# Attention's running sums over seven block pairs, with suffix sums on GpSimd, and late modulation sums on column quarters

## The reference

```python
z = einsum('bhqd,bhkd->bhqk', qb, kb) * scale
strict = s_idx < t_idx
log_keep = where(strict, log_sigmoid(-z), 0.0)
later = cumsum(log_keep, axis=3, reverse=True) - log_keep
att = where(strict, exp(log_sigmoid(z) + later), 0.0)
```

## Time and profile before

| what | value |
|---|---|
| median of 3 runs | 1100.38 us |
| lowest and highest run | 1097.2 and 1100.89 us |
| span of the profiled execution | 1095.7 us, 4.7 us below the median |
| TensorE, VectorE, ScalarE, GpSimd busy | 94, 61, 30 and 15% of the span |
| mean granted clock of TensorE | 0.994 of full speed |
| traffic with HBM | 254 GB/s over the span |

### The profile page before, as it was taken

The page is one execution under the profiler, slowest core; times in us unless marked ns, Lnnn a source line. Parts: engine busy times, 40 slices in busy tenths (PEclk is TensorE's granted clock), DMA queues, the critical chain, the costliest instruction groups (busy, mean ns, idle before and its releaser), DMA issues.

```text
span 1095.7 us, 18202 instructions
## 1 busy us (share of the span) xinstructions
PE 1028.6 (94%) x7403; PEld 591.1 (54%) x7403; DVE 665.0 (61%) x1131; ACT 326.2 (30%) x500; POOL 167.4 (15%) x220
## 2 busy tenths in 40 slices
PE   3999999999999999999998999999999999889895
PEld 1588588755557677768884444444334333333332
DVE  2478768444457443238347777777776665666666
ACT  4342462366652223365351111111111101110114
POOL 0100000322220011264500200000000000001003
PEclk9999999999999999999999999999999999999998
DMA  9676303205320004243439999999999999999994
GB/s 342 245 242 217 136 28 127 77 13 180 115 77 2 3 4 157 72 155 123 172 122 407 376 396 401 400 402 399 407 404 408 404 404 395 405 396 402 411 423 196
DMA packets 67732, 275.22 MB, mean 251 GB/s; under 512 B 7742, under 2 KB 17256, under 8 KB 43098
## 3 DMA queue, kind: packets, MB, share of 16 engines
q1 hardware_dynamic: 62976, 263.84, 62.4%
q10 hardware_dynamic: 2218, 6.52, 1.6%
q0 software_dynamic: 2480, 4.01, 1.3%
HBM read 274.26 MB, written 4.21 MB: 254 GB/s over the span
## 4 chain that ended last, share of the span: by engine, by line
PE 45%; SPq 25%; DVE 13%; DMA 7%; ACT 5%; issue 3%; POOL 1%; DVEq 0%; ACTq 0%
SPq L476 17%; PE ps L2211 8%; SPq L480 5%; PE ps L2230 4%; PE ps L1878 3%; DMA ring<-in_w_in 3%; DMA arena<-in_w_up 2%; SPq L484 2%; PE ps L2195 2%; PE ps L1859 2%; DMA arena<-in_w_mod 2%; PE ps L1867 2%; PE ps L1979 2%; PE ps L1860 1%; PE ps L1861 1%
## 5 line engine op out<-in xcount | busy, mean ns | idle before, releaser
L1544 DVE TENSOR_TENSOR arena<-arena,ps 128x1024 f32<-128x1024 f32 x124 | 145.5, 1215 | 52.9 <-PE ps L2195 52.9
L2211 PE MATMUL ps<-arena 128*64 128x512 f32 x672 | 152.9, 596 | 12.0 <-DMA arena<-in_w_up 11.2
L2211 PEld LDWEIGHTS ps<-arena 128*64 128x64 f32 x672 | 47.5, 137 | 105.5 <-issue 99.8
L1054 ACT ACTIVATE results<-ps,ST 64x512 fp32r<-64x512 f32 x64 | 43.8, 685 | 182.8 <-PE ps L2230 182.4
L2211 PE MATMUL ps<-ring,arena 128*64 128x512 f32 x352 | 79.9, 597 | 6.9 <-DMA ring<-in_w_up 5.5
L1047 ACT ACTIVATE arena<-ps 128x256 f32<-128x256 f32 x32 | 12.3, 385 | 234.7 <-PE ps L2211 234.7
L1720 PE MATMUL ps<-h_upper,w_upper 128*128 128x512 f32 (+1 forms) x184 | 73.7, 401 | 4.8 <-POOL h_lower_first L604 4.6
L2230 PE MATMUL ps<-arena 128*64 128x512 f32 x336 | 76.7, 598 | 1.3 <-DMA arena<-in_w_down 1.3
L1554 DVE SCALAR_TENSOR_TENSOR results<-ps,ST,results 64x512 fp32r<-64x512 f32 x64 | 48.0, 749 | 47.4 <-ACT results L1054 46.9
L2195 PE MATMUL ps<-results,back 128*128 128x512 f32 x248 | 73.7, 419 | 0.0
L1722 PE MATMUL ps<-h_upper,w_lower 128*128 128x512 f32 (+1 forms) x184 | 72.1, 392 | 0.0
(11 more groups left out here) (424 smaller groups left out, 1866.7 us busy)
## 6 DMA issues: line engine op xcount, KB each, us to landing
arena<-in_w_up SPq DMA_DIRECT2D x84, 1024.0 KB, 28.1
ring<-in_w_up SPq DMA_DIRECT2D x44, 1024.0 KB, 27.7
ring<-in_w_down SPq DMA_DIRECT2D x11, 2048.0 KB, 32.4
arena<-in_w_down SPq DMA_DIRECT2D x11, 2048.0 KB, 31.4
arena<-in_w_down SPq DMA_DIRECT2D x20, 1024.0 KB, 27.2
ring<-in_w_mod SPq DMA_DIRECT2D x6, 2048.0 KB, 9.1
arena<-in_w_mod SPq DMA_DIRECT2D x6, 2048.0 KB, 9.5
ring<-in_w_in SPq DMA_DIRECT2D x6, 2048.0 KB, 8.4
```

Source lines behind the costliest of these rows:

```text
L1544: TT(two_banks(acc[:, t, :]), two_banks(acc[:, t, :]), ps[:, BACK_BANK[t]:BACK_BANK[t] + 2, :], ALU.add).then_inc(back_added, 1)
L2211: last = mm(ps[64 * hf:64 * hf + 64, UP_BANK, :].rearrange("p (m n) -> p m n", m=2), hgT[:, k, :], up_pair(u, k)[:, :, 256 * hf:256 * hf + ...
```

## The change

Running sums. After the masks, GpSimd adds to the off-diagonal part of key block 2 the block 3, and to that of block 1 the new block 2 (`suffix_sums`), each after a wait for its own instruction before. Then block 1 holds, for the queries behind it, the sum of blocks 1 to 3. `sums` needs only the pair (`j`, `j`) and the next one: for `j` = 0 with `nones` on block 1, for `j` = 1 and 2 with a third matrix `-before` (-1 where the row lies strictly ahead of the column), which takes off what the triangular product of the enlarged block counted too much. Seven pairs, 14 products per head. ScalarE makes the third matrix from the constants.

Late modulation. Each accumulator is multiplied with 32 columns of ones only, into a quarter of 32 partitions of one of two banks; VectorE copies both banks to `late_rows`; TensorE, between the first two parts of Gram group 0, turns them by eight transposes of 128x128; VectorE picks every 32nd column and adds the bias in two small additions, after the first three steps of group 0. The separate addition of the bias goes away.

```diff
-        tri_r = sb("tri_r", [P, 2, P], F32R)
+        tri_r = sb("tri_r", [P, 3, P], F32R)
...
+        late_rows = acc_l[0:2]
...
-        LATE_BANK = (2, 3, 4, 5, 2, 3, 2, 3)
+        LATE_BANK = (2, 3)
...
+            def suffix_sums(buf, h):
+
+                for j, step in ((2, 1), (1, 2)):
+                    pool.wait_ge(sp_added, 2 * h + step)
+                    v, n = buf[:, OFF[j] + P:OFF[j] + WID[j]], WID[j + 1]
+                    nc.gpsimd.tensor_tensor(v, v, buf[:, OFF[j + 1]:OFF[j + 1] + n], ALU.add).then_inc(
+                        sp_added if step == 1 else sp_masked, 1)
...
-                    diag(e_buf[i], sp_masked)
+                    diag(e_buf[i], sp_added)
+                    suffix_sums(e_buf[i], 2 * p + i)
...
-            A(tri_r[:, 1, :], K("nones"), ACT.Copy).then_inc(lora_tri, 1)
+            A(tri_r[:, 1, :], K("nones"), ACT.Copy)
+            A(tri_r[:, 2, :], K("before"), ACT.Copy, scale=-1.0).then_inc(lora_tri, 1)
...
-            own = eb[:, 0:2048].rearrange("p (j q n) -> p j q n", j=4, q=4)
-            dve.wait_ge(av_all, NH)
-            for j in range(NH):
-                dve.wait_ge(lcol_done, j + 1)
-                TT(own[:, j % 4], ps[:, LATE_BANK[j], :].rearrange("p (q n) -> p q n", q=4),
-                   K("ident").rearrange("p (o n) -> p o n", o=1).broadcast_to((P, 4, P)), ALU.mult).then_inc(lcol_evac, 1)
-                dve.wait_ge(lcol_evac, j + 1)
-                ins = nc.vector.tensor_reduce(modc[:, 4 * j:4 * j + 4].rearrange("p (q o) -> p q o", o=1), own[:, j % 4], AX, ALU.add)
+            dve.wait_ge(lcol_done, 2)
+            for b in range(2):
+                CP(late_rows[b], ps[:, LATE_BANK[b], :]).then_inc(lcol_evac, 1)
+
+            def late_sums_in():
+
+                dve.wait_ge(lcol_done, 3)
+                turned = psf[:, 512 * LATE_BANK[0]:512 * LATE_BANK[0] + 1024].rearrange("p (b q c x) -> p b q c x", b=2, q=4, x=32)
+                of = lambda a: a.rearrange("p (b c q) -> p b q c", b=2, c=4)
+                for b in range(2):
+                    ins = TT(of(modc)[:, b], turned[:, b, :, :, 0], of(V("bl", 0, 32))[:, b], ALU.add)
+                ins.then_inc(lcol_evac, 1)
...
-                link(TT(modc, modc, V("bl", 0, 32), ALU.add))
+                dve.wait_ge(lcol_evac, 3)
...
+                if f == 0:
+                    late_sums_in()
...
-                    for jj in range(j, NT):
+                    for jj in range(j, min(j + 2, NT)):
                         o = 1536 * (h % 2) + OFF[j] + P * (jj - j)
+                        left = 0 if jj == j else (1 if j == 0 else 2)
                         for sp in (sp_hi[h % 2], sp_lo[h % 2]):
-                            last = mm(psf[:, o:o + WID[jj]], tri_r[:, 0 if jj == j else 1, :],
+                            last = mm(psf[:, o:o + WID[jj]], tri_r[:, left, :],
...
-            def late_sum(j):
-                if j >= 4:
-                    earlier = max(i for i in range(j) if LATE_BANK[i] == LATE_BANK[j])
-                    pe.wait_ge(lcol_evac, earlier + 1)
-                mm(ps[:, LATE_BANK[j], :], K("ones"), acc_l[j], start=True, stop=True).then_inc(lcol_done, 1)
-
-            for j in range(6):
-                late_sum(j)
+            for b in range(2):
+                for q in range(4):
+                    last = mm(ps[32 * q:32 * q + 32, LATE_BANK[b], :], K("ones")[:, 0:32], acc_l[4 * b + q], start=True, stop=True)
+                last.then_inc(lcol_done, 1)
...
-                        pe.wait_ge(lcol_evac, NH)
+                        pe.wait_ge(lcol_evac, 3)
...
-                    late_sum(6)
-                    late_sum(7)
+                    for b in range(2):
+                        pe.wait_ge(lcol_evac, b + 1)
+                        for q in range(4):
+                            last = tr(ps[:, LATE_BANK[b], P * q:P * q + P], late_rows[b][:, P * q:P * q + P], ident)
+                    last.then_inc(lcol_done, 1)
```

More of the change, by code:

```diff
@@ L321, in build @@
         tok_src, tr_done, tr_act, tr_dve = sem("tok_src"), sem("tr_done"), sem("tr_act"), sem("tr_dve")
-        sp_rounded, sp_split = sem("sp_rounded"), sem("sp_split")
+        sp_rounded, sp_split, sp_added = sem("sp_rounded"), sem("sp_split"), sem("sp_added")
         z_done, log_ready, sp_ready, sp_masked, cum_done, att_ready, att_masked, av_all, ysb_ready = (
```

## The result

The changed kernel takes 1104.63 us (median), the kernel before 1099.6 us beside it: a ratio of 1.0048, with a 95% interval of 1.0034 to 1.0062. It is slower by 5 us, where 1.6 us less was forecast, and outside the range. The profiled execution has a span of 1099.8 us.

A forecast was written before the change was run, and what follows sets the result against it. Bound: chains of waits in attention and behind it, carried one to one through the expert stage. Attention +2.6 and late modulation -4.2 give -1.6 us, a span of about 1094.1; applied to the median, 1098.8 us, range 1095.6 to 1102.8.

The forecast's parts named there:

- TensorE's clock falls: Rival, attention: 2.1 us idle before the second head's sums halves the clock, 10.4 us more in four pairs, 1109; chance 0.07.
- The adds: Attention, GpSimd: two adds per head put 1.16 us (0.98 to 1.35) on the second head's chain, nothing on the first's.
- the upper row: Attention, GpSimd: 2.1 ns per column plus 0.19 us per start gave 1.19 us for both adds; 1.0 was taken.
- the proportion to one larger instruction: Attention, GpSimd: scaling the 128x512 in-place product (1.09 us) to 384 columns gave 0.82 us for both adds.
- The sums: Attention, TensorE: 14 products per head instead of 20 save 0.5 us per pair of heads, 0.57 at most.
- The net of a pair: Attention: 1.16 - 0.5 = +0.66 us per pair of heads (0.41 to 0.89), +2.6 us over four.
- The late part: From last values products to attention output product: 8.2 us instead of 12.45, taken as -4.2 us.
- Eight transposes: Late modulation, TensorE: eight transposes of 128x128 cost twice 0.87 = 1.74 us.
- the boundaries between groups: Late modulation, TensorE: five new boundaries at 0.06 us each would cut the gain from 4.3 to 4.0 us.
- the first head stays off the chain: Attention: first head's adds end by 253.84, before ScalarE's rounding at 254.01, costing nothing; rival that they are late: 1102.8, chance 0.09.
- the quarters run side by side: Late modulation, TensorE: eight products onto 32 rows take 1.85 us; rival that they don't: 6.9 us, total 1103.9, chance 0.05.
- VectorE's copies and the output weights are hidden: Late modulation: copies (1.4 us) fit under the first Gram group's 1.75; output weights land at 6.7 us, needed at 8.2.

The follow-up runs named there:

- the version kept busy: Changed kernel plus five products of 256 columns without use between the first and second head's sums; 1098.16 us, ratio 0.9985 to the kernel before.
- the late part alone: Changed kernel with the attention part undone (ten block pairs, no adds on GpSimd), late modulation kept; 1095.27 us, ratio 0.9967 to the kernel before.

## Why the prediction was wrong

The step that failed is that the sum gave TensorE's longer idle time no cost. The prediction held it only in the rival *TensorE's clock falls*, at a chance of 0.07, because the gap is nearer to the harmless one. The gap was foreseen (2.1 us; it is 2.52) and its consequence priced, but two rows, one at 1.44 us without a fall and one at 3.42 with one, were read as if the fall came somewhere between and nearer to the upper one. The runs show falls after 1.82 us, and none after 2.51 us in another pair; the idle time alone does not decide, and a chance of 0.07 was far too low. The size: 3.85 - 2.31 = 1.54 us in each of three pairs, and in the first pair 0.8 in the sums (3.12 instead of 2.32) and 0.8 in the gate products (3.44 instead of 2.62), 6.2 us in all. With four times the 0.68 us of a pair at full clock, below, that is 8.9 of the 9.1 us by which attention is longer in the trace. That rival's price, half of the gate products at 0.50, put the fall behind the sums; it lies mostly in them.

The rest of the working held in its mechanism. With the clock kept, the kernel comes out at 1098.16 us, 1.6 us below before (2.9 to 0.5 by the interval), which is the forecast -1.6. The close agreement is partly luck: three terms were mis-sized, the first two cancel within 0.1 us over the four pairs, and by the chain of waits the sum is nearer to -2.1.

- The adds take 1.38 us from masks to rounding, 1.36 more than before, against 1.16 forecast and a bound of 1.35. The groups by form say 457 and 732 ns: the upper row, 2.1 ns per column and 0.19 us for a start, was right, and the proportion to one larger instruction was not. The Trainium skill (GPSIMD Engine Reference, 3.1) gave an estimated 0.84 us by the column from an instruction of 2048; the 1.19 us measured here decide, and the difference is the two starts.

```profile
L623 POOL TENSOR_TENSOR arena<-arena 128x256 f32<-128x256 f32 x8 | 5.9, 732 | 0.6
L623 POOL TENSOR_TENSOR arena<-arena 128x128 f32<-128x128 f32 x8 | 3.7, 457 | 0.7
```

- The sums lose 0.67 us, not 0.5: 2.98 against 2.31. The starts read in narrow windows of the merged timeline gave about 0.03 us too little for each of the six products. The net of a pair is 0.68 us (25.79 against 25.11 us from the version kept busy), forecast 0.66.
- The late part wins 4.85 us, not 4.2. Eight transposes take 1.02 us, not 1.74: the eight records in the earlier trace rows were taken for four transposes of two records each, but a transpose leaves one record, a product of 32-bit floats two. With the transposes at 1.02 the forecast's own terms give 7.46 us; the 7.6 measured leave 0.14 for the boundaries between groups, which it had put at 0.3 at most.

Borne out: the first head stays off the chain (its adds end before ScalarE's rounding at 257.24 comes free), the quarters run side by side (1.85 us), the masks don't change, VectorE's copies and the output weights are hidden (no step of theirs is in the chain behind the values products), and what attention loses reappears at the expert stage.

What stays open is why, at an equal idle time, one pair keeps its clock and the next does not. Other stages show the same, at shorter idle times: all nine traces have an idle time of 0.84 us ahead of narrow products between 411 and 434 us and one of 0.68 us between 565 and 588 us, and within 3 us behind each the clock fell to 0.50 in three of the nine (the late part alone and the version kept busy show both falls). So the row at 1.44 us without a fall gave no bound either. The Trainium skill (TensorE: Matmul & The Clock Gate, Part 1) says of the rise of the clock, as work begins, that its point varies from run to run. The falls here vary too, of which that sentence does not speak, and no run was made to shift the pairs against the clock.

## What to carry to other kernels

When a change makes an engine ahead of TensorE slower, and TensorE's own work there shorter, look at the new idle time first, not at the sum of the durations: here 20 products without use made the kernel 6.5 us faster. If an idle time opens between dense products, put work that is queued behind it into it; the same change loses 0.5% without that and wins 1% with it. Where the trace has only two idle times, a harmless one and a harmful one, a gap in between belongs into the range and not into the tail; and one trace is not enough to call a gap harmless.

## What the runs showed of the hardware that was not expected

- The clock fell from 2.4 to 1.2 GHz after 1.82 us without products, in the midst of a stage in which TensorE is otherwise busy, in three pairs of four; after 2.5 us in two of four in one kernel and in four of four in another. In none of these nine falls did it fall in the idle time itself: seven came within 0.5 us of the work's return, the two in first pairs 1.2 and 1.6 us after it.
- Within 3 us behind idle times of 0.84 us and 0.68 us, in two stages of narrower products, the clock fell in three traces of nine each.
- A fall in attention costs about 1.5 us here: 14 products 3.85 instead of 2.31, 20 products 4.53 instead of 3.00.
- GpSimd's add costs 0.18 us to start and 2.15 ns per column (457 and 732 ns at 128 and 256 columns).
